# A router that sorts tokens to experts: one pass over all tiles, or a choice tile by tile with the instructions for the eight largest and their places

## The reference

```python
lg = xf @ w_rg + b_rg                      # 4 group logits of each token
g_star = argmax(lg)
le_g = (xf @ w_re + b_re).reshape(-1, 4, 8)[row, g_star]
top_v, top_i = top_k(le_g, 2)              # two experts of that group
w_tok = softmax(top_v) * softmax(lg)[g_star]
eid = g_star * 8 + top_i
y = sum over both experts e of w_tok[e] * (silu(x @ w_gate[e]) * (x @ w_up[e])) @ w_down[e]
```

## Time and profile before

| what | us |
|---|---|
| median of 3 runs (lowest, highest) | 910.57 (909.29, 913.3) |
| the profiled execution | 911.5 |
| its span, first to last instruction | 909.7 |
| TensorE busy | 770.4 |
| VectorE busy | 373.1 |
| ScalarE busy | 223.4 |
| GpSimd busy | 173.2 |

### The profile page before, as it was taken

The page is one execution under the profiler, slowest core; times in us unless marked ns, Lnnn a source line. Parts: engine busy times, 40 slices in busy tenths (PEclk is TensorE's granted clock), DMA queues, the critical chain, the costliest instruction groups (busy, mean ns, idle before and its releaser), DMA issues.

```text
span 909.7 us, 11093 instructions
## 1 busy us (share of the span) xinstructions
PE 770.4 (85%) x4293; PEld 526.7 (58%) x4293; DVE 373.1 (41%) x742; ACT 223.4 (25%) x477; POOL 173.2 (19%) x271
## 2 busy tenths in 40 slices
PE   0999999998989989999898879999991599988710
PEld 0555778584756667777666667754551456554500
DVE  1100598999778861030044532222237222221135
ACT  2101223252256651251243410001010012211121
POOL 1075625210100013000024200010000213221112
PEclk9999999999999999999999989999995599998965
DMA  8759535240210015522134289011137289999663
GB/s 276 160 4 298 143 90 134 96 128 1 64 53 2 1 30 158 166 66 70 47 93 140 80 241 363 1 49 79 47 146 281 84 316 412 407 400 398 241 229 115
DMA packets 91126, 138.95 MB, mean 153 GB/s; under 512 B 29209, under 2 KB 64153, under 8 KB 89911
## 3 DMA queue, kind: packets, MB, share of 16 engines
q1 hardware_dynamic: 71967, 103.77, 33.2%
q0 software_dynamic: 11392, 32.71, 12.3%
q10 hardware_dynamic: 7712, 1.72, 1.0%
HBM read 132.00 MB, written 21.14 MB: 168 GB/s over the span
## 4 chain that ended last, share of the span: by engine, by line
PE 69%; DVE 8%; DMA 8%; issue 6%; SPq 4%; ACT 2%; POOL 1%; POOLq 0%; DVEq 0%; ACTq 0%
PE ps L1839 17%; PE ps L2011 13%; PE ps L2254 6%; DMA keep<-w_up 6%; PE ps L1855 5%; PE ps L2323 4%; PE ps L1918 3%; SPq L640 3%; PE ps L2054 2%; PE ps L2029 2%; PE ps L2042 2%; PE ps L2339 1%; PE ps L1831 1%; PE ps L1899 1%; PE ps L2202 1%
## 5 line engine op out<-in xcount | busy, mean ns | idle before, releaser
L2011 PE MATMUL ps<-xT,keep 128*128 128x288 f32 x512 | 126.9, 407 | 0.8 <-ACT h L1178 0.4
L2011 PEld LDWEIGHTS ps<-xT,keep 128*128 128x128 f32 x512 | 96.5, 190 | 27.3 <-ACT h L1178 0.6
L1839 PE MATMUL ps<-xT,arena 128*128 128x288 f32 x384 | 95.4, 407 | 0.0
L1309 DVE SCALAR_TENSOR_TENSOR cv<-keep,cv 128x512 f32<-128x512 f32 x120 | 83.6, 747 | 1.4
L1839 PEld LDWEIGHTS ps<-xT,arena 128*128 128x128 f32 x384 | 72.1, 190 | 19.2
L2254 PE MATMUL ps<-arena,xT 128*128 128x512 f32 x128 | 55.5, 593 | 1.8 <-issue 1.8
L2323 PE MATMUL ps<-keep,mgT 128*64 128x256 f32 x288 | 45.7, 427 | 8.9 <-DMA keep<-w_up 7.6
L1855 PE MATMUL ps<-mgT,xT 128*128 128x512 f32 (+1 forms) x128 | 45.7, 521 | 1.1 <-ACT xT L1014 1.1
L2254 PEld LDWEIGHTS ps<-arena,xT 128*128 128x128 f32 x128 | 24.1, 190 | 31.4 <-issue 31.4
L2323 PE MATMUL ps<-arena,mgT 128*64 128x256 f32 x256 | 39.5, 409 | 3.1 <-DMA arena<-w_up 2.9
L792 ACT ACTIVATE mgT<-ps 64x512 f32<-64x512 f32 x56 | 33.2, 592 | 32.2 <-PE ps L1899 31.6
(11 more groups left out here) (377 smaller groups left out, 1283.9 us busy)
## 6 DMA issues: line engine op xcount, KB each, us to landing
arena<-w_down SPq DMA_DIRECT2D x21, 512.0 KB, 16.4
keep<-w_gate SPq DMA_DIRECT2D x18, 512.0 KB, 11.5
keep<-w_up SPq DMA_DIRECT2D x18, 512.0 KB, 17.2
keep<-w_in SPq DMA_DIRECT2D x16, 512.0 KB, 3.8
arena<-w_gate SPq DMA_DIRECT2D x14, 512.0 KB, 8.4
arena<-w_up SPq DMA_DIRECT2D x14, 512.0 KB, 12.8
h<-x_prompt SPq DMA_DIRECT2D x8, 512.0 KB, 5.4
arena<-w_in SPq DMA_DIRECT2D x8, 512.0 KB, 6.4
```

The costliest lines, as they stand in the source:

```text
L1309: V.scalar_tensor_tensor(cv[:, c, 0:SEQ], aP[:, c, k:k + SEQ], wdw[:, c, k:k + 1], cv[:, c, 0:SEQ], ALU.mult, ALU.add).then_inc(s_tap[c], 1)
L1839: last = mm(tokens(j)[:, b, :], weights(k), halves(x[:, k, :])[:, b, :], start=k == 0, stop=k == n_k - 1)
L2011: last = mm(out[:, 0:half], wmg[n // 2 % 3][:, k, :], xT[:, k, (n % 2) * half:(n % 2 + 1) * half], start=k == 0, stop=k == KD - 1, skip_gr ...
```

## The change

The choice is made tile by tile (`choose`), each behind the logits of its tile. The instruction `max` gives the eight largest of a row in order, `max_index` their places. A group of 4 logits is padded to 8; the logits of the other groups get a large negative number, and the two best of the 32 left are the two experts. A running sum over tiles (`so_far`) takes the place of the totals. All tables of ones and zeros are bf16, as are the matrices of ones. The rank matmul sums ranks and earlier tiles in the accumulator. The number of further blocks is a shift by 6, the prefix sum one scan instruction, the block of a slot a shift by 6. The inversion carries the token's number as two bf16 numbers, one half made by VectorE and one by ScalarE. The softmax weights are computed behind `slots_of`.

The lines here are cut to the core; lines removed are mostly those that the function above shows.

```diff
@@ ScalarE, behind the squares of the tiles
+            act.wait_ge(s_onehot, 1)
+            nc.scalar.activation(codes[:, :, 1, :], in_block, ACT.Copy, scale=q_id).then_inc(s_lo, 1)
@@ VectorE
-                give(V.tensor_tensor(lg[r, i, :], slot(j)[r, 0:NR], brow[r, :], ALU.add), j)
+                V.tensor_tensor(lg[r, i, 0:NG], slot(j)[r, 0:NG], brow[r, 0:NG], ALU.add)
+                give(V.tensor_tensor(lg[r, i, 8:], slot(j)[r, NG:NR], brow[r, NG:NR], ALU.add), j)
+                result_of(dve, j)
+
+            def choose(i):
+
+                r, t = on(h, i), slice(i * NE, (i + 1) * NE)
+                st.do(V.max(best_g[r, i, :], lg[r, i, 0:8]))
+                st.do(V.max_index(which_g[r, i, :], best_g[r, i, :], lg[r, i, 0:8]))
+                st.do(V.tensor_scalar(rt[r, 0, 0:NE], g_no[r, :], which_g[r, i, 0:1], NEG, ALU.not_equal, ALU.mult))
+                st.do(V.tensor_tensor(rt[r, 1, 0:NE], lg[r, i, 8:], rt[r, 0, 0:NE], ALU.add))
+                st.do(V.max(best[r, i, :], rt[r, 1, 0:NE]))
+                st.do(V.max_index(which[r, i, :], best[r, i, :], rt[r, 1, 0:NE]))
+                st.do(V.tensor_scalar(first[r, t], e_no[r, :], which[r, i, 0:1], None, ALU.is_equal))
+                st.do(V.scalar_tensor_tensor(chosen[r, t], e_no[r, :], which[r, i, 1:2], first[r, t], ALU.is_equal, ALU.add))
+                if i:
+                    V.tensor_tensor(so_far[r, (i + 1) * NE:(i + 2) * NE], so_far[r, t], chosen[r, t], ALU.add).then_inc(s_chosen, 1)
+                else:
+                    V.tensor_copy(so_far[:, NE:2 * NE], chosen[:, 0:NE]).then_inc(s_chosen, 1)
+                V.tensor_scalar(second[r, t], e_no[r, :], which[r, i, 1:2], None, ALU.is_equal)
+                st.do(V.tensor_scalar(row_at.rearrange("p (n t) -> p n t", n=2)[r, :, i], which[r, i, 0:2], float(BR), None, ALU.mult))
+                if i == QT - 1:
+                    st.do(V.tensor_copy(so_far[NS_TOK:, NT * NE:], so_far[NS_TOK:, QT * NE:NT * NE]))
...
                 logits(i - 2)
                 normed_turned(i - 1)
+                choose(i - 2)
             merged_out(4)
             logits(2)
             normed_turned(3)
             scaled(4)
+            choose(2)
             logits(3)
             normed_turned(4)
+            choose(3)
             logits(4)
+            choose(4)
...
-            first_best(gm, v3(1, NG), lgG, NG, cidx[:, 0:NG], gsel)
...
-            over = cells(NE, MAX_OVER)
...
-            for step in (1, 2, 4, 8, 16):
...
+            take(dve, J_POS)
+            at, total = slot(J_POS)[:, 0:NT * NE], slot(J_POS)[:, 512:512 + NE]
+            st.do(V.tensor_scalar(n_over, total, -1.0, 0.0, ALU.add, ALU.max))
+            st.do(V.tensor_scalar(n_over, n_over, 6, None, ALU.arith_shift_right))
+            st.do(V.tensor_tensor_scan(run[:, 1:], one_e, n_over, 0.0, ALU.mult, ALU.add))
+            st.do(V.scalar_tensor_tensor(shift, run[:, 0:NE], float(BR), over_at, ALU.mult, ALU.add))
+            st.do(V.scalar_tensor_tensor(by_tile(jump), by_tile(at), float(BR), shift.unsqueeze(1).to_broadcast([P, NT, NE]), ALU.is_ge, ALU.mult))
+            give(V.tensor_tensor(at_place, jump, at, ALU.add), J_POS)
+            result_of(dve, J_POS)
+            st.do(V.tensor_tensor(prod, rt[:, 20:22, 0:NT * NE], at_place.unsqueeze(1).to_broadcast([P, 2, NT * NE]), ALU.mult))
+            st.do(V.tensor_reduce(row_no, prod.rearrange("p c (t e) -> p (c t) e", e=NE), AX.X, ALU.add))
+            st.do(V.tensor_tensor(slot_i, row_no, row_at, ALU.add))
+            st.do(V.tensor_scalar(block_i, slot_i, 6, None, ALU.arith_shift_right))
+            st.mark(V.scalar_tensor_tensor(row_no, block_i, -float(BR), slot_i, ALU.mult, ALU.add))
+            V.tensor_tensor(in_block, block_id.unsqueeze(1).to_broadcast([P, 2 * NT, NBLK]), wide_at(block_i, NBLK), ALU.is_equal).then_inc(s_onehot, 1)
+            st.sync()
+            V.tensor_tensor(in_row, rows64.unsqueeze(1).to_broadcast([P, 2 * NT, BR]), wide_at(row_no, BR), ALU.is_equal)
+            dve.wait_ge(s_onehot, 1)
+            V.tensor_tensor(codes[:, :, 0, :], in_block, wide_at(token_hi, NBLK), ALU.mult).then_inc(s_onehot, 1)
...
@@ TensorE
-            pe.wait_ge(s_sub, 3)
+            pe.wait_ge(s_chosen, QT)
             claim(pe, J_POS)
-            for weights, at in ((tri, 0), (onesC[:, :], NT * NE)):
...
+            mm(at[:, 0:NT * NE], ones_b, so_far[:, 0:NT * NE], start=True, stop=False, skip_group_check=True)
+            mm(at[:, 0:QT * NE], tri_b, chosen[:, 0:QT * NE], start=False, stop=True, skip_group_check=True)
+            pe.wait_ge(s_chosen, NT)
+            mm(at[:, QT * NE:NT * NE], tri_b[0:NS_TOK, :], chosen[0:NS_TOK, QT * NE:], start=False, stop=True, skip_group_check=True)
+            fill(mm(at[:, 512:512 + NE], ones_b, so_far[:, NT * NE:], start=True, stop=True), J_POS)
...
+            for x in range(2 * NT):
+                r = on(h, x % NT)
+                for half in range(2):
+                    last = mm(slot(J_INV)[half * BR:(half + 1) * BR, 0:2 * NPAIR].rearrange("p (c a) -> p c a", c=2), in_row[r, x, :],
+                              codes[r, x, :, :].rearrange("p c (a b) -> p c a b", b=2)[:, :, :, half], start=x == 0, stop=x == 2 * NT - 1)
```

## The result

The changed kernel takes 895.84 us (median of four runs, 894.7 to 896.74) where the kernel before takes 910.84 on the same chip: ratio 0.9832 [0.9807, 0.9857]. The profiled execution took 895.58 us (span 893.8, mean granted clock 0.946), 15.9 less than the profiled one of before.

A forecast was written before the change was run, and what follows sets the result against it. The router, a serial string of small VectorE instructions, was taken to delay the fixed-length weight stream. Router -16.8 and gather +1.3 gave -15.5 us: 911.5 to 896.0 profiled, 895.1 by the median, say 895; range 891 to 901.

The forecast's parts named there:

- (a): Preparation and choices of tiles 0 and 1: they lie in VectorE's idle time and cost nothing.
- (b): `choose(2)` and `choose(3)` between the logits: last logits start 0.5 us later, tile 4's logits finish +1.0 us later.
- (c): From tile 4's logits to the matrix TensorE needs: 7.2 us become 2.0, softmax weights moved away, -5.2 us.
- (d): Rank matmuls: 2.8 us in fp32 become 0.5 in bf16, with only two waiting for tile 4, -2.3 us.
- (e): From ranks to the one-hot rows on VectorE: 13.0 us become 5.4, -7.6 us.
- (f): Inversion matmuls: 5.4 us for 40 fp32 instructions become 1.7 for 20 bf16 ones, -3.7 us.
- The term for the search: Twelve eight-largest and place instructions on the router's path at 0.30 us each: +1.0 us, ends -0.8 and +3.4.
- The gather: First gather of token rows behind `slots_of`: meets weight loads still on the queue, +1.3 us, ends 0 and 3.2.
- R3: Rival: expert stage's end is set by something not starting with the first freed home; 908 to 910 us, chance 0.03.
- R1: Rival: dearer search, gather, inversion and scan, together +5.6 us, 900.7 us; chance 0.17 with partial forms.
- R2: Rival: cheaper search (-1.8), no gather contention (-1.3), cheaper inversion (-0.8), 891.2 us; chance 0.08.
- R4: Rival: eight-largest and place instructions are slow ones of fixed length; 916.6 us at 2.1 us each, chance 0.02.

The follow-up runs named there:

- before_weights_moved: The kernel before with only the softmax weights (six VectorE instructions and their wait) moved behind `slots_of`: 910.07 us, ratio 0.9982.
- fp32_tables: The changed kernel with one-hot rows, blocks and codes in fp32 instead of bf16, rank matmuls still bf16: 895.83 us, ratio 0.9821.
- filler15: The changed kernel with 15 further VectorE products of 320 elements, read by nothing, once the ranks are there: 903.67 us, ratio 0.991.
- late_choice: The changed kernel with all five choices behind the last tile's logits instead of each behind its own: 902.34 us, ratio 0.9894.
- first_gather_warm4_7: The changed kernel with 4 filling matmuls before and 7 behind the inversion, loads of blocks 7 and 8 held for the first gather: 901.14 us.
- warm5_14: The changed kernel with 5 unread filling matmuls on TensorE before the inversion and 14 behind it: 896.62 us, ratio 0.9806.
- changed (third): The changed kernel unaltered, run a third time as yardstick on another chip: 896.02 us, ratio 0.9827.
- changed (again): The changed kernel unaltered, run once more as yardstick on another chip: 895.92 us, ratio 0.9781.
- first_gather_warm: The changed kernel with 5 filling matmuls before and 14 behind the inversion, loads of blocks 7 and 8 held for the first gather: 897.46 us.
- warm4_7: The changed kernel with 4 unread filling matmuls on TensorE before the inversion and 7 behind it: 892.15 us, ratio 0.9792.
- gather_first: The changed kernel with the loads of blocks 7 and 8 held until all four first gathers have landed: 895.55 us, ratio 0.9811.
- first_gather: The changed kernel with the loads of blocks 7 and 8 held until the first gather alone has landed: 893.99 us, ratio 0.9781.

## Why the prediction was right, step by step

Forecast 895, range 891 to 901; measured 895.84.

(a) held: nothing of the preparation shows. (b) The last logits start 0.7 late against 0.5, and their sums 1.4 late against 1.0, counted from the start of `h`. `choose(2)` takes 679.85 to 682.30, 2.45 us, near the 2.2 plus the dearer search. (c) 686.19 to 688.46 = 2.3, predicted 2.0. (d) 0.45 against 0.5. (e) 688.91 to 694.15 = 5.2 against 5.4, instruction by instruction. (f) 694.15 to 695.31 = 1.2 against 1.7: the size was right within its bounds, the reason given with it, the two-byte type, was not whole: the fp32 tables showed 1.8 us for the type, and the other 2.4 came with the alternating halves. (g) 1.35 against 1.3. The term for the search was meant as 12 times 0.30. From start to next start, one eight-largest takes 0.19 to 0.23 and one place 0.26 to 0.30, a third of a microsecond in all over the 0.22 price, not +1.0. By the rule cited for it the place is two instructions; the trace agrees, 0.09 and 0.16. That each costs a whole small instruction, 0.44 together, it does not bear out. Another half microsecond of that +1.0 went into instructions with a scalar read from memory, 0.24 instead of 0.18 us, four in each choice, which I had not listed.

Sum -17.8 against -16.8 for the router: right within 1 us. That the total came out within 1 us is in part luck: this execution's late start (+1.3), longer stream (+0.8), shorter tail (-1.2) and the router's extra 1.0 were none of them forecast and cancel to 0.1. From the first addition to the last `w_up`, 238.5 us became 222.5, a gain of 16.0 against the 15.5 forecast.

The gather: +1.2 against +1.3, and the experiment with the hold shows that it is the loads. It is no fixed toll. In the two other profiled executions of the changed kernel `slots_of` came 1.5 us later (a gain of 16.4 in the router), the gather took 4.50 and 4.83, and the first transposes started only 0.2 and 0.5 us later. So the last microsecond and a half taken out of the router bought a few tenths: it brought the gather into the loads. The Trainium skill ("DMA: Bandwidth & Descriptors", "SWDGE vs HWDGE vs iDMA") has the engine alternate between software-made and hardware-made queues; that 5.74 lies between 4.54 with the loads away and 7.9 in the full stream agrees. That a gather doesn't stand at the end of the line is seen in the full stream of the kernel before, where loads issued beside the gathers of 7.9 us took more than twice as long to land:

```profile
keep<-w_up SPq DMA_DIRECT2D x14, 512.0 KB, 17.4
```

The 5.74 alone could not tell: the loads were nearly over, and waiting for their end would have cost about the same. The put of rows never waited for the softmax weights: 5.8 us of cover, 4 predicted.

The step on which all rests was that the expert stage is a stream of fixed length that starts with the first freed home. Stretches from there to the landing of the last `w_up`, one profile each:

```
kernel                 first addition   first home free   last w_up lands   home to w_up   addition to w_up
before                         619.62            729.76            858.11          128.4              238.5
before_weights_moved           619.75            727.24            856.04          128.8              236.3
fp32_tables                    632.15            725.43            854.58          129.2              222.4
filler15                       621.31            721.31            849.88          128.6              228.6
late_choice                    619.64            720.15            848.81          128.7              229.2
first_gather_warm4_7           631.75            720.09            851.82          131.7              220.1
warm5_14                       621.76            715.88            844.99          129.1              223.2
changed (third)                621.65            715.54            844.22          128.7              222.6
changed (again)                621.45            715.22            843.31          128.1              221.9
first_gather_warm              620.53            714.60            845.57          131.0              225.0
changed                        620.92            714.21            843.41          129.2              222.5
warm4_7                        621.46            712.46            841.02          128.6              219.6
gather_first                   620.75            711.61            841.67          130.1              220.9
first_gather                   619.83            710.93            839.79          128.9              220.0
```

In the ten kernels and repeats without held loads the start moves by 17 us and the length only between 128.1 and 129.2. R3 is out by this. With held loads the length is 128.9 to 131.7: there a start gained in front is partly given back, and by up to 3 us where the filling was added. R1 was not there: no term of it came true. R2 was there in part, in the search (0.25 on average against 0.30) and the inversion (1.1 against 1.6). R4 is out: no instruction of the new kinds takes over 0.25 us.

What stays open: why the clock fell at 450 us; whether the hold gains; how much of the 3.9 us is the filling's; and whether the order of halves alone makes the inversion shorter, since no run changed it by itself.

## What to carry to other kernels

When the chain shows a long piece without an engine and the transfers stand still beside it, price every small instruction in it, find what starts the next full stretch, and check that its length doesn't depend on where it starts; then a gain at the start comes out at the end. Work that depends on one tile goes behind that tile, into time in which the engine waits anyway: that gave about 6.5 of the 15 us here, with the same instructions. Expect the transfer that now starts earlier to meet what was on the queue until then: 1.2 us here, which ate most of the last 1.5 us of the gain.

## What the hardware did that I had not expected

- Matmul records of 64 columns that alternate between the two halves of the array start every 0.073 us on average in fp32, those in one half every 0.133, at the same granted clock of 0.50. The two of a pair start 0.007 us apart.
- Filling TensorE raised the granted clock to 1.00 at 693 us and made its next visits shorter: the first transposes from 1.97 to 1.16 or 1.04 us, and with fourteen matmuls behind the inversion the pair from 5.56 to 3.67. The smaller filling ended 3.9 us below the changed kernel; fourteen gained nothing (896.62 against 895.92).
- The clock falls at different points in executions of the same kernel. In the third run of the changed kernel it was down for all of 680 to 685,

```profile
680.00:685.00 5.00, 4.67 (x24) 4.42 (x24) 3.18 (x17) 0.00 (x0) 0.00 (x0) 0.50 1.02 397
```

  and the logits of tile 3 took 3.63 us instead of 1.98, which put `slots_of` 1.5 us later, from the first addition, than in the first. The second run shows the same 3.63.
- A scan over 32 elements takes 0.23 us, an addition of as many 0.19.
